# Two first tiles reordered, and five summing matmuls fewer per tile, in an eight-core encoder kernel

## What is computed

```
for layer in range(2):
    g = norm_g[layer]                      # pre/post mixer, pre/post ffn
    h = rmsnorm(x, g[0])
    h = mixer_ab(h, ...) if layer % 2 == 0 else mixer_c(h, ...)
    x = x + rmsnorm(h, g[1])
    h = swiglu(rmsnorm(x, g[2]), w_gate, w_up, w_down)   # 1024 -> 2816 -> 1024
    x = x + rmsnorm(h, g[3])
```

## Time and profile before

| | us |
|---|---|
| median of 3 runs | 4064.33 (4059.5 to 4079.43) |
| profiled execution, its own time | 4059.64 |
| its span on the slowest core (7) | 4058.0 |
| spans of the eight cores | 4044.7 to 4058.0 |
| PE busy | 3926.5 (97%), 19879 matmuls |
| DVE busy | 1857.9 (46%) |
| ACT busy | 1733.5 (43%) |
| POOL busy | 245.8 (6%) |
| mean granted clock of TensorE | 0.987 to 0.990 of full speed by core |

### The profile page before, as it was taken

One profiled execution on the slowest core, in us unless ns is written; L12 is line 12 of the kernel. 1 busy time (PEld: TensorE's weight loads), 2 busy tenths in 40 slices (PEclk: granted clock), 3 DMA queues, 4 the chain that ended last, 5 costly groups with the idle time before them and its releaser, 6 DMA issues.

```text
span 4058.0 us, 58466 instructions; the slowest of 8 cores (4044.7 to 4058.0 us)
## 1 busy us (share of the span) xinstructions
PE 3926.5 (97%) x19879; PEld 1941.1 (48%) x19879; DVE 1857.9 (46%) x3228; ACT 1733.5 (43%) x2846; POOL 245.8 (6%) x542
## 2 busy tenths in 40 slices
PE   7878999999999999999999999999999999999998
PEld 3333444444444444444444445544445655456655
DVE  5622662372463455345336237336336354363432
ACT  6412552362453454445335336435335444353432
POOL 0000220010010000001001002001001000010000
PEclk9899999999999999999999999999999999999999
DMA  8898688654454454455455446555446666456665
GB/s 271 253 221 232 178 221 205 172 191 153 151 188 154 144 178 163 158 168 175 151 171 170 154 143 217 182 172 177 151 161 199 202 206 206 155 189 202 202 210 190
DMA packets 187394, 748.93 MB, mean 185 GB/s; under 512 B 22720, under 2 KB 29888, under 8 KB 182080
## 3 DMA queue, kind: packets, MB, share of 16 engines
q1 hardware_dynamic: 185504, 719.49, 54.1%
q0 software_dynamic: 1600, 25.69, 4.4%
HBM read 723.08 MB, written 73.40 MB: 196 GB/s over the span
## 4 chain that ended last, share of the span: by engine, by line
PE 90%; DMA 5%; DVE 1%; issue 1%; ACT 1%; SPq 0%; DVEq 0%; POOL 0%; ACTq 0%; POOLq 0%
PE PS L493 90%; DMA XR<-wsrc 4%; DMA RG<-wbf 1%; SPq L535 0%; ACT VN L506 0%; DVE RG L531 0%; DMA X<-wsrc 0%; DVE XG L522 0%; DVE ARENA L511 0%; DVE TT L511 0%; DVE H L511 0%; DVE X L511 0%; ACT L526 0%; ACT GB L504 0%; ACT L506 0%
## 5 line engine op out<-in xcount | busy, mean ns | idle before, releaser
L493 PE MATMUL PS<-XG,RG 128*128 128x512 bf16 (+4 forms) x12800 | 2555.7, 360 | 63.8 <-DMA RG<-wbf 26.6
L493 PEld LDWEIGHTS PS<-XG,RG 128*128 128x128 bf16 x12800 | 1254.5, 98 | 1325.5 <-issue 102.2
L493 PE MATMUL PS<-ARENA,RG 128*128 128x512 bf16 (+2 forms) x4816 | 980.9, 362 | 2.4 <-DVE ARENA L511 2.4
L493 PEld LDWEIGHTS PS<-ARENA,RG 128*128 128x128 bf16 x4816 | 471.5, 98 | 489.9 <-issue 4.7
L506 ACT ACTIVATE SQO<-PS 128x512 bf16<-128x512 f32 (+2 forms) x416 | 233.6, 565 | 822.2 <-PE PS L493 816.3
L511 DVE TENSOR_TENSOR SQO<-SQO 128x512 bf16<-128x512 bf16 (+2 forms) x351 | 142.2, 405 | 879.7 <-ACT SQO L506 866.7
L506 ACT ACTIVATE H<-PS,CST 128x512 f32<-128x512 f32 (+2 forms) x416 | 270.4, 652 | 9.3 <-PE PS L493 7.4
L511 DVE TENSOR_TENSOR H<-H,R 128x1024 f32<-128x1024 f32 (+2 forms) x208 | 231.3, 1139 | 84.3 <-ACT R L527 84.3
L506 ACT ACTIVATE TT<-PS 128x512 f32<-128x512 f32 (+2 forms) x190 | 107.4, 566 | 354.1 <-PE PS L493 353.2
L511 DVE TENSOR_TENSOR ARENA<-PS,TT 128x512 bf16<-128x512 f32 (+2 forms) x183 | 118.7, 649 | 279.7 <-PE PS L493 252.1
L511 DVE TENSOR_TENSOR ARENA<-PS,GB 128x512 bf16<-128x512 f32 (+2 forms) x183 | 118.4, 647 | 275.5 <-PE PS L493 236.4
(11 more groups left out here) (80 smaller groups left out, 1961.5 us busy)
## 6 DMA issues: line engine op xcount, KB each, us to landing
RG<-wbf SPq DMA_DIRECT2D x711, 512.0 KB, 3.5
RG<-wbf SPq DMA_DIRECT2D x200, 704.0 KB, 4.5
RG<-wbf SPq DMA_DIRECT2D x104, 768.0 KB, 5.2
y<-X SPq DMA_DIRECT2D x36, 512.0 KB, 8.4
XR<-xin SPq DMA_DIRECT2D x64, 264.0 KB, 5.9
wbf<-RG SPq DMA_DIRECT2D x32, 512.0 KB, 9.7
XR<-wsrc SPq DMA_DIRECT2D x15, 1024.0 KB, 13.0
CB<-wsrc SPq DMA_DIRECT2D x13, 1024.0 KB, 12.4
```

What stands on the lines that cost most here:

```text
L493: return lambda e: e.matmul(out, lhsT, rhs, start=start, stop=stop)
```

## The change

The two first tiles get a new written order. The first norm of tile 1 is done like that of tile 0. Slabs of V and Z stay in place for both tiles. V of tile 0 runs block by block of the input over four banks at once. V, Z of tile 1 stand ahead of `mix(0)`, U of tile 1 behind `out0(0)` and its chain. To make room, slabs, U, pooled Z and products of the two tiles live for a while in parts of `X[0]`, `H`, `CV`, `GB` and `TT`, `R` and `VN`. Seven FFN chunks of tile 0 are followed by the same seven of tile 1 out of the same slabs (two of them in `R` and `VN`), and 15 pairs follow. `down0(0)` is in one piece, and `down0(1)` uses its last four slabs first. Casts begin ahead of the first pair, every 22 us of matmul time until the last down slab's write-back is issued, then every 8. Tile 2's first normed input goes to `CB[1]` and a part of `X[2]`, so that `n1(2)` can stand ahead of `down0(1)`; chunks 4 to 7 of `cin(0)` stand behind `zvu(2)`. A write-back is issued at the next `acquire`, behind the last main matmul written so far. The instructions that make `VN` go head by head in all tiles and are tracked per head; for tiles 0 and 1 every second head is made on DVE. The tables of norms 1 and 2 change as shown. The planner has one shared pipe for DMAs with other rates. `chain0` of tiles 0 and 1 is in class 0.

The core of the diff; left out are the same functions with the new arguments passed through (`zvu` is now `zvu_v`, `vnorm`, `zvu_z` and `zvu_u`, one behind the other):

```diff
-CAST_PACE = 10.0
+CAST_PACE = 8.0
...
-SQ_LEVEL = {"n": 3, 1: 2, 2: 0, 3: 3, 4: 3, 5: 3, 6: 3, 7: 3}
+SQ_LEVEL = {"n": 3, 1: 3, 2: 1, 3: 3, 4: 3, 5: 3, 6: 3, 7: 3}
...
-        pipe = {"hw": 0.0, "sw": 0.0}
+        pipe = [0.0]
...
-                p = "sw" if e == "pool" else "hw"
-                rate = 120e3 if e == "pool" else 300e3
-                pipe[p] = max(pipe[p], now) + o.size / rate
-                o.end = pipe[p] + 1.8
+                rate = 118e3 if e == "pool" else 319e3
+                pipe[0] = max(pipe[0], now) + o.size / rate
+                o.end = pipe[0] + 1.8
...
-        bVN = bufs(4)
+        bVN = [bufs(4) for _ in range(4)]
...
+        def stage_set(j):
+            if j >= CC0:
+                return (0, 5)
+            if j < FF0:
+                return (0, 1, 2)
+            return (0, 2) if j < FF0 + 3 else (0, 2, 3, 4) if j < FF0 + 9 else (2, 3, 4)
...
-            if not cast_todo or cast_clock[0] < CAST_PACE:
+            if not cast_todo or cast_clock[0] < (CAST_PACE if bWBF[DN0 + 7].w else 22.0):
...
+        wb_todo = []
+
+        def write_back():
+            while wb_todo:
+                j, dst, ap, pages = wb_todo.pop(0)
+                k = rnext("wb", 4)
+                after = Buf()
+                after.w = P.main_pe
+                dma("sp", dst, ap, f"wb{k}", 256 * SLAB_COLS[j], reads=pages + [after], writes=[bWBF[j], bWBS[k]], cls=0)
+
+        def acquire(j, home=None):
+            write_back()
             u = SLAB_COLS[j]
             n = u // 256
-            if ring_pos[0] + n > NRP:
-                ring_pos[0] = 0
-            p0 = ring_pos[0]
-            ring_pos[0] += n
-            pages = bRG[p0:p0 + n]
-            ap = RING[:, p0 * 256:p0 * 256 + u]
+            if home is None:
+                if ring_pos[0] + n > NRP:
+                    ring_pos[0] = 0
+                p0 = ring_pos[0]
+                ring_pos[0] += n
+                pages = bRG[p0:p0 + n]
+                ap = RING[:, p0 * 256:p0 * 256 + u]
+            else:
+                ap, pages = home
...
-                k = rnext("wb", 4)
-                dma("sp", flat_ap(wbf), ap, f"wb{k}", 256 * u, reads=pages, writes=[bWBF[j], bWBS[k]], cls=0)
+                wb_todo.append((j, flat_ap(wbf), ap, pages))
...
+        def xgn(t):
+            if t == 2:
+                cb = flat2(CB[1])
+                return [cb[:, 528 * c:528 * c + 528] for c in range(7)] + [X[2][:, 3, :].bitcast(BF16)], \
+                       [bCB[1][528 * c // 512:(528 * c + 527) // 512 + 1] for c in range(7)] + [[bX[2][3]]]
+            return [XG[t % 2][:, c, :] for c in range(8)], [[b] for b in bXG[t % 2]]
...
+            banks = [next_bank() for _ in offs]
+            if t == 0:
+                for kc in range(7):
+                    pe([mm(b, kc, o) for b, o in zip(banks, offs)], 512, need(kc), [bBK[b] for b in banks])
+            for jc, (b, o) in enumerate(zip(banks, offs)):
+                ks = range(7 * (t == 0), 8)
+                pe([mm(b, kc, o) for kc in ks], 512, (), [bBK[b]], per=[need(kc) for kc in ks])
                 act(Vt[:, jc, :], PS[:, b, 0:512], AF.Gelu_apprx_tanh, 512, [bBK[b]], bV[jc], cls=0, tab="gelu")
...
+        def vnorm(t):
+            nv = TILE_T[t] // 128 + int(t == HALO_TILE)
+            for h in range(4):
+                for jc in range(nv):
                     k = jc * 4 + h
                     v = Vt[:, jc, h * 128:(h + 1) * 128]
-                    act(VN[:, jc, h * 128:(h + 1) * 128], v, AF.Identity, 128, bV[jc] + [bRV, bNM], [bVN[jc]],
+                    if h % 2 and t < 2:
+                        ts(VN[:, jc, h * 128:(h + 1) * 128], v, RV[:, k:k + 1], ALU.mult, 128, bV[jc] + [bRV, bNM],
+                           [bVN[jc][h]], s2=NM[:, k:k + 1], op1=ALU.add)
+                        continue
+                    act(VN[:, jc, h * 128:(h + 1) * 128], v, AF.Identity, 128, bV[jc] + [bRV, bNM], [bVN[jc][h]],
                         scale=RV[:, k:k + 1], bias=NM[:, k:k + 1])
...
+            got = {}
+            for q, i in enumerate(order):
+                j = i // per_slab
+                if j not in got:
+                    got[j] = have.get(j) or acquire(slab0 + j, home.get(j))
+                slab, pages = got[j]
...
-        n1_first()
-        zvu(0, load_wsp)
+        home = lambda ap, bb, c: (flat2(ap[:, c:c + 2, :]).bitcast(BF16), bb[c:c + 2])
+        n1_first(0)
+        v01 = two_slabs(VC0)
+        zvu_v(0, load_wsp, v01)
         load_x(1, 0, XR1, bXR1)
-        n1(1, XR1, bXR1)
-        mix(0)
-        out0(0)
-        chain0(0)
-        zvu(1)
-        mix(1)
-        for f in range(2):
-            ffn0_chunk(0, f)
-        out0(1)
-        chain0(1, XR1, bXR1)
-        for f in range(2, 11):
-            ffn0_chunk(0, f)
+        n1_first(1, XR1, bXR1)
+        vnorm(0)
+        z01 = two_slabs(ZC0)
+        zvu_z(0, z01)
+        zvu_u(0, home(X[0], bX[0], 4))
+        rt1 = CVA[:, :].bitcast(BF16).rearrange("p (g w) -> p g w", g=4)
+        brt1 = [bCV[0], bCV[0], bCV[1], bCV[1]]
+        ab0 = flat2(X[0][:, 6:8, :]).bitcast(BF16).rearrange("p (g w) -> p g w", g=4)
+        ab0 = [ab0[:, g, :] for g in range(4)]
+        bab0 = [[bX[0][6 + g // 2]] for g in range(4)]
+        zvu_v(1, None, v01)
+        zvu_z(1, z01, rt1, brt1)
+        mix(0, ab0, bab0)
+        vnorm(1)
+        out0(0, {0: home(H, bH, 4), 1: home(H, bH, 6)}, ab=ab0, bab=bab0)
+        chain0(0, cls=0)
+        u1 = GTA[:, :].rearrange("p (g w) -> p g w", g=4)
+        zvu_u(1, None, u1, bGB + bTT)
+        mix(1, u=u1, bu=bGB + bTT, f2=RS1, bf2=bRS1)
+        out0(1, {}, rt1, brt1)
+        chain0(1, XR1, bXR1, cls=0)
+        LEAD = 7
+        spare = {0: (flat2(Rt), bR), 1: (flat2(VN), flat(bVN))}
+        first = [ffn0_chunk(0, f, acquire(FF0 + f, spare.get(f))) for f in range(LEAD)]
+        for f in range(LEAD):
+            ffn0_chunk(1, f, first[f])
         cast_todo.extend(range(NDIRECT, NSLAB))
-        for f in range(11, NFF):
+        for f in range(LEAD, NFF):
             ffn0_chunk(1, f, ffn0_chunk(0, f))
-        for f in range(11):
-            if f < 8:
-                down0(0, Hc1, bHc1, range(f, f + 1))
-            ffn0_chunk(1, f)
+        kept = down0(0, Hc1, bHc1)
         load_x(2)
-        n1_stats(2)
-        down0(1)
-        cin(0, range(8))
-        cin_edges(0)
-        n1_apply(2)
+        n1(2)
+        down0(1, have={j: kept[j] for j in range(4, 8)}, order=(7, 6, 5, 4, 0, 1, 2, 3))
+        cin(0, range(4))
         for n in range(2, NT + 1):
             c, b = n - 1, n - 2
             if n < NT:
                 zvu(n)
+            if n == 2:
+                cin(0, range(4, 8))
+                cin_edges(0)
             cin(c, range(0, 3))
             if n < NT:
                 mix(n)
```

More of the change, by code:

```diff
@@ L639, in acquire, with n1_first @@
             return ap, pages
-        def n1_first():
-            HW = tile_width(0) // 2
+        def n1_first(t, src=None, bsrc=None):
+            HW = tile_width(t) // 2
+            src, bsrc = (XR, [[b] for b in bXR]) if src is None else (src, bsrc)
             for c in range(0, 8, 2):
@@ L688, in zvu, with two_slabs, zvu_v @@
         def zvu(t, after_v=None):
+            zvu_v(t, after_v)
+            vnorm(t)
+            zvu_z(t)
+            zvu_u(t)
+        def two_slabs(j):
+            return [acquire(j + s) for s in range(2)]
+        def zvu_v(t, after_v=None, slabs=None):
             T = TILE_T[t]
             halo = t == HALO_TILE
-            TW = T + 32 if halo else T + 16
-            xg, bxg = XG[t % 2], bXG[t % 2]
-            ic, bic = ICE[t % 2], bICE[t % 2]
+            xg, bxg = xgn(t)
             nj = T // 128
[L695 to L699, removed]
+            slabs = slabs or two_slabs(VC0)
+            v3 = [slab.rearrange("p (k c) -> p k c", k=4) for slab, _ in slabs]
+            vpages = [pages for _, pages in slabs]
             offs = [8 + 128 * jc for jc in range(nj)] + ([T + 32] if halo else [])
             nv = len(offs)
[L702 to L705, removed]
-                pe(fns, 512, (), [bBK[b]], per=[[bxg[kc]] + (vpages[kc // 4] if kc % 4 == 0 else []) for kc in range(8)])
+            mm = lambda b, kc, o: mmop(PS[:, b, 0:512], xg[kc][:, o:o + 128], v3[kc // 4][:, kc % 4, :], kc == 0, kc == 7)
+            need = lambda kc: bxg[kc] + (vpages[kc // 4] if kc % 4 == 0 else [])
+            banks = [next_bank() for _ in offs]
[5 more added lines that the diff above has]
+                pe([mm(b, kc, o) for kc in ks], 512, (), [bBK[b]], per=[need(kc) for kc in ks])
                 act(Vt[:, jc, :], PS[:, b, 0:512], AF.Gelu_apprx_tanh, 512, [bBK[b]], bV[jc], cls=0, tab="gelu")
@@ L797, in mix @@
                 if halo:
                     stt(fb[:, T:T + 1], PS[:, b, T:T + 1], gv, CST[:, C_BSH + h:C_BSH + h + 1], ALU.mult, ALU.add, 1,
[L799 to L807 removed]
+                        [bBK[b], bCST], bfb, cls=0)
```

(28 more changed lines are left out.)

149 lines of the change are left out of this document (66 added, 83 removed).

## The result

The changed kernel took 4032.46 us (median of 6 runs), the one before 4081.74 beside it; the ratio is 0.9913, 95% interval 0.9886 to 0.9940: faster by 0.9%, where 1.8% was forecast, and 2 us outside the range. The profiled execution took 4033.18 us with a span of 4031.6, 26.4 less than before; that is 0.65%, inside the interval. (In some executions one die ran at a lower clock and the time was longer, 4496 us for instance; all ratios and ranges of runs in this document leave those out.)

A forecast was written before the change was run, and what follows sets the result against it. It took the first 480 us to be held up mainly by slab loads and casts, the rest bound by TensorE. 4059.6 less 61 at the start and 11 from fewer sums gave 3988 us, range 3955 to 4030.

The forecast's parts named there:

- the casts at a pace of 8: Casts one per 8 us behind 480 us: DMA share 86%, costing nothing, at worst 10 us of stalls.
- the fewer sums: Norms 1 and 2, tiles 2 to 12: five fewer summing matmuls per tile gain 10.8 us, bounds -20 and 10.8.
- (b): V, Z, U, mix and out of tiles 0 and 1: 14 us of PE idle, bounds 5 and 28.
- the clock: Slower PE clock after stalls at the start: 14 us lost, against 32 before.
- (a): First loads of the kernel, unchanged: PE idle 15 us, as in the first 20 us before.
- (c): Seven FFN chunks of tile 0, same seven of tile 1, then fifteen pairs: 8 us idle, bounds 0 and 20.
- (d): down(0), no longer mixed with chunks of tile 1, short of DMA time: 16 us idle, bounds 0 and 26.
- (e): down(1) with four slabs kept, then four chunks of cin(0): 2 us idle, bounds 0 and 8.
- The planner's model: Shared DMA pipe in the planner reorders instructions everywhere: could give 10 us or take as much, taken as zero.
- 77 us of DMA relief: DMA time saved before tile 2, 34 us of loads and 43 of casts: ceiling of the gain from this side.
- rival 2: Sums come late because the adds make PE wait: +31 us, 4019 us; chance 0.06.
- Rival 1: The start stays bound, DVE or the down slabs replacing the FFN loads: 4020 us; chance 0.15.

The follow-up runs named there:

- e4: Changed kernel with the planner's old model of transfers and old order of events put back; 0.9969 of the time of the kernel before.
- e10: Kernel before with only cast timing changed: one per 22 us until the last down slab is written back, then per 8; 0.9952 of before.
- e7: Changed kernel without casting DMAs, the second layer reading the first layer's bf16 slabs (wrong weights); 0.9826 of the kernel before.
- e8: Kernel before without casting DMAs, the second layer reading the first layer's bf16 slabs (wrong weights); 0.9848 of the kernel before.
- e9: Changed kernel with one cast per 14 us in place of 22, then per 10 in place of 8; 0.9933 of the kernel before.
- e2: Changed kernel with the table entries of norms 1 and 2 put back to levels 2 and 0; 0.9953 of the kernel before.
- e1: Kernel before with only the table entries of norms 1 and 2 changed, to levels 3 and 1; 1.0041 of the kernel before.

## Why the prediction was right in direction and wrong in size

The steps that failed are three: the casts at a pace of 8, taken at nothing, cost 19 us; the fewer sums, taken at 10.8, gave about 4; and the start gave 44 in place of 61, since DVE in (b) and the clock cost more. By the spans, 72 us were forecast (61 and 11) and 26.4 came: 44.2 up to mix 2, 18.6 lost in the next round, 0.8 won behind it.

- *Direction, and where.* Right: faster, the gain at the start, PE bound behind.
- *Start, (a).* Right: the first V matmul at 19.30, and (a) kept its 15 us.
- *(b)* failed: 14 us of idle predicted, 19.8 measured from 20 to 126 us, and PE's granted clock was 0.74 from 100 to 120; the first FFN chunk came at 126 in place of some 107 (the prediction's pace and idle, without its clock term). Of these 19 us 6 are idle, the rest is the slower clock. DVE was the bound from 100 to 120 us, tighter than I took it: busy 19.95 of 20 us.

```profile
100.00:120.00 20.00, 11.21 (x43) 4.41 (x42) 19.95 (x29) 11.56 (x17) 0.00 (x0) 0.74 0.58 203
```

PE stood for 8.8 us at sums of tile 0, in front of out(1), whose input DVE also had still to make:

```profile
104.00 1.01 PE L499 MATMUL PS<-SQC,ONES 128*128 128x512 bf16 x2 [3.91 <-DVE SQC L517]
107.61 0.58 PE L499 MATMUL PS<-SQC,ONES 128*128 128x512 bf16 x1 [2.59 <-DVE SQC L517]
110.47 0.59 PE L499 MATMUL PS<-SQC,ONES 128*128 128x512 bf16 x1 [2.29 <-DVE SQC L517]
```

- *(c)* right: 126 to 287 us had 5.6 us of idle against 8. *(d)* right in place: down(0) took 62 us for 38 of work, 19.2 of them waits for the copies of late slabs, 16 predicted; DVE in turn waited 30.6 us there for fp32 slabs to land. The longest of the three:

```profile
329.05 3.23 PE L499 MATMUL PS<-CB,RG 128*128 128x512 bf16 x8 [11.56 <-DVE RG L537]
```

  *(e)* 5 us where 2 was taken. Tile 2's V came at 417 us, 398 forecast: 64.6 us of idle in place of 55, and 23 us of slower clock in place of 14. In all 44 us won in place of 61.
- *The planner's model: zero* was wrong by some 24 us in the change's favour (e4). The forecast of the start came as near as it did by luck: without this term 21 us would have been won up to mix 2 (medians).
- *The bytes.* The 77 us of DMA relief were no bad ceiling, but its parts were not alike: 29 us at mix 2 come with the casts' timing alone (e10), and with no casts at all the new order, 10.7 MB less and the new planner together give 3.7, or 7.4 by the medians (e7, e8).
- *Casts at a pace of 8: "nothing, at worst 10"* is the step that failed worst. The share was forecast well (86%, measured 90), the conclusion from a mean share below 100% was wrong: the round behind mix 2 took 341.7 us, and 322.0 without casts (e7); with one cast per 10 us it took 330.3 (e9). 18.6 us longer than before.
- *Fewer sums: 10.8 us* was mis-sized. The matmuls went, but a round became 0.8 us shorter, not 1.1. Of this 0.4 is the table's (e2) and 0.5 the planner's (e4); DVE's patch of CB came later, 0.57 us of wait per round: the mechanism of rival 2, at a buffer it did not name. From the mix of tile 3 to the end the table of sums is worth about 4 us (3213.7 in e2, 3209.8 after, medians of the cores; e2 ran on the slower chip). With the waits for GT that the VN order brought to round 9-10, only 0.8 us in all was won behind round 2-3 (3.1 by the medians).
- The rule of 358 GB/s, which the prediction takes from the Trainium skill (DMA: Bandwidth & Descriptors, Specifications), would have moved the estimate to 3979, away from the result. No run here tests it further.

Rival 1 gave the start's mechanism (DVE in (b), down slabs in (d)) and 4020. What is open: why e1 lost 20 us up to the mix of tile 3 (13 by the medians). From mix 2 on its waits for slabs are 7.8 us; up to 7 us can be the chip's, and no run separated the cast timing, which the shifted plan moves, from the adds. Open too is which part of the planner's change carries its share, and what it would do alone.

## What to carry to other kernels

Moving background transfers out of a full stretch pays only what their new place does not charge: price them by taking them out altogether, in both places. A mean DMA share does not tell whether a stretch is free: here 79% cost nothing in the round behind mix 2 and 90% cost 19 us. Look at the full stretches in it and at how long a load takes to land. A sum on a matrix engine that works in the planned order is worth its matmul only if the vector engine that feeds it and its neighbours has time just there. And when the order of instructions comes from a planner, take its model back by itself: here it carried half of what the new order seemed to give.

## What was not expected of the hardware

- A slab of 512 KB landed in 3.6 us (median) without casts beside it and in 8.5 with casts at 38% of the engines' time, the total share being 90%; in the kernel before, at 79%, it was 5.9 (475 to 700 us).
- One stall of 11.56 us cost more than itself: the eight matmuls behind it took 3.23 us where eight take 1.89. The granted clock was 0.58 in the mean over them, so most of this time was at the lower level of 1.2 GHz.
